# A decoder trunk on one core: the first blocks of x turned one by one, and the first products placed ahead of x's second piece

## What is computed

```python
for l in range(DEPTH):                       # DEPTH 2, D 1024, S 256 rows, float32
    h = rms_norm(x, g_mix[l])
    z = h @ w_in[l]                          # all heads' projections and four gates
    # A: sliding window, 8 query and 2 key heads, rotary; B: latent attention;
    # C: three dilated windows; M: cross-attention into rms_norm(mem)
    ...
    x = x + einsum(gates * y, w_out[l])      # y: the four branches through w_branch
    u = rms_norm(x, g_mlp[l]) @ w_up[l]
    x = x + square(relu(u)) @ w_down[l]
```

## Time and profile before

| | us |
|---|---|
| median of 3 runs | 1241.1 (1241.07 to 1242.55) |
| the profiled execution, whole | 1239.82 |
| its span (what the profile's times count from) | 1238.0 |
| PE busy | 1227.8 |
| DVE busy | 783.5 |
| ACT busy | 701.3 |
| POOL busy | 157.4 |

### The profile page before, as it was taken

One profiled execution on the slowest core, in us unless ns is written; L12 is line 12 of the kernel. 1 busy time (PEld: TensorE's weight loads), 2 busy tenths in 40 slices (PEclk: granted clock), 3 DMA queues, 4 the chain that ended last, 5 costly groups with the idle time before them and its releaser, 6 DMA issues.

```text
span 1238.0 us, 17641 instructions
## 1 busy us (share of the span) xinstructions
PE 1227.8 (99%) x6296; PEld 1018.7 (82%) x6296; DVE 783.5 (63%) x1223; ACT 701.3 (57%) x1087; POOL 157.4 (13%) x127
## 2 busy tenths in 40 slices
PE   8999999999999999999999999999999999999998
PEld 7888888877778888888888888888777888888887
DVE  5857768875556664444567576788655567554454
ACT  6667766654554465545566677666544454644543
POOL 5612334200000000000021223342000000000000
PEclk9999999999999999999999999999999999999999
DMA  9545444455437556565555454444543455555652
GB/s 250 199 135 154 144 136 146 152 167 147 130 112 228 173 178 184 192 180 189 191 162 183 138 156 136 137 136 154 170 134 122 132 196 182 171 191 183 187 186 102
DMA packets 111221, 202.62 MB, mean 164 GB/s; under 512 B 10016, under 2 KB 18720, under 8 KB 111136
## 3 DMA queue, kind: packets, MB, share of 16 engines
q1 hardware_dynamic: 106128, 194.64, 50.7%
q10 hardware_dynamic: 4464, 6.82, 1.7%
q0 software_dynamic: 544, 0.03, 0.1%
HBM read 200.41 MB, written 1.05 MB: 163 GB/s over the span
## 4 chain that ended last, share of the span: by engine, by line
PE 98%; DMA 1%; ACT 0%; issue 0%; ACTq 0%; DVE 0%
PE ps_d L1355 23%; PE ps_d L1357 22%; PE ps_d L1356 22%; PE ps_b L1355 5%; PE ps_b L1356 5%; PE ps_b L1357 5%; PE ps_b L1435 5%; PE ps_b L1389 5%; PE ps_b L1408 4%; PE ps_b L1414 2%; DMA xs<-in_x_dram 1%; PE ps_d L1330 0%; ACT k_c L998 0%; ACT L1042 0%; ACT w_hi L927 0%
## 5 line engine op out<-in xcount | busy, mean ns | idle before, releaser
L1092 DVE TENSOR_TENSOR w_lo<-raw,w_hi 128x1024 fp32r<-128x1024 f32 (+4 forms) x381 | 450.9, 1187 | 309.3 <-ACT w_hi L927 308.0
L927 ACT ACTIVATE w_hi<-raw 128x1024 fp32r<-128x1024 f32 (+4 forms) x381 | 392.1, 1029 | 448.2 <-PE ps_d L1357 349.9
L1355 PE MATMUL ps_d<-w_hi,h_hi 128*128 128x512 f32 (+3 forms) x704 | 285.8, 406 | 0.0
L1357 PE MATMUL ps_d<-w_hi,h_lo 128*128 128x512 f32 (+3 forms) x704 | 267.7, 380 | 0.0
L1356 PE MATMUL ps_d<-w_lo,h_hi 128*128 128x512 f32 (+3 forms) x704 | 266.8, 379 | 0.0
L1355 PE MATMUL ps_d<-w_hi,r_hi 128*128 128x512 f32 (+1 forms) x552 | 219.3, 397 | 0.0
L1357 PE MATMUL ps_d<-w_hi,r_lo 128*128 128x512 f32 (+1 forms) x552 | 214.1, 388 | 0.0
L1356 PE MATMUL ps_d<-w_lo,r_hi 128*128 128x512 f32 (+1 forms) x552 | 213.8, 387 | 0.0
L1355 PEld LDWEIGHTS ps_d<-w_hi,h_hi 128*128 128x128 f32 x704 | 132.6, 188 | 26.1 <-issue 4.6
L1357 PEld LDWEIGHTS ps_d<-w_hi,h_lo 128*128 128x128 f32 x704 | 132.3, 188 | 25.6
L1356 PEld LDWEIGHTS ps_d<-w_lo,h_hi 128*128 128x128 f32 x704 | 132.9, 189 | 18.9
(11 more groups left out here) (156 smaller groups left out, 1277.8 us busy)
## 6 DMA issues: line engine op xcount, KB each, us to landing
raw<-in_w_in_dram SPq DMA_DIRECT2D x151, 512.0 KB, 3.5
raw<-in_w_up_dram SPq DMA_DIRECT2D x64, 512.0 KB, 3.6
raw<-in_w_down_dram SPq DMA_DIRECT2D x64, 512.0 KB, 3.7
raw<-in_w_branch_dram SPq DMA_DIRECT2D x32, 512.0 KB, 3.7
raw<-in_m_w_kv_dram SPq DMA_DIRECT2D x16, 512.0 KB, 4.7
raw<-in_w_out_dram SPq DMA_DIRECT2D x16, 512.0 KB, 3.6
early<-in_b_gate_dram ACTq DMA_DIRECT2D x16, 256.0 KB, 3.6
raw<-in_w_in_dram SPq DMA_DIRECT2D x8, 384.0 KB, 3.5
```

Source lines behind the costliest of these rows:

```text
L927: nc.scalar.activation(w_hi[:, u % RING, 0:kn, 0:cn], raw[:, u % RAW, 0:kn, 0:cn], ACT.Copy).then_inc(hi_split, 1)
L1092: nc.vector.tensor_tensor(w_lo[:, u % RING, 0:kn, 0:cn], raw[:, u % RAW, 0:kn, 0:cn], w_hi[:, u % RING, 0:kn, 0:cn].bitcast(F32), ALU.subt ...
L1355: nc.tensor.matmul(o, hi[:, a["c"], cut], wh, start=a["first"], stop=False)
L1357: last = nc.tensor.matmul(o, lo[:, a["c"], cut], wh, start=False, stop=a["last"])
```

## The change

x's first two blocks are turned and evicted as two items instead of one of two blocks. Its second piece is issued by SyncE, right behind unit 0. All of x's row norms and the memory's get an order number 7 us later; several assumed times change; the first unit of the value projection C0 is cut so that it stands behind the first of query A; and the idle turns are 14 and 8 instead of 24 and 16.

```diff
-    free = {"PE": 0.0, "ACT": 0.0, "DVE": 0.0, "POOL": 14.5, "DMA": 2.4}
+    free = {"PE": 0.0, "ACT": 0.0, "DVE": 0.0, "POOL": 14.5, "DMA": 1.2}
...
-                   since=8.0, q=q, src=source, tt=tt, l=l, **k)
+                   since=13.0, q=q, src=source, tt=tt, l=l, **k)
...
-        def x_turns(c0, c1, dest, gain, came, jobs_needed, order=None):
-            for c in range(c0, c1, 2):
-                turn(("x", jobs_needed), came, c, 2, P, dest, "split", gain, l, order=order,
-                     since=0.0 if jobs_needed else (5.0, 5.6, 8.4)[min(c // 2, 2)])
+        def x_turns(c0, c1, dest, gain, came, jobs_needed, order=None, m=2):
+            for c in range(c0, c1, m):
+                turn(("x", jobs_needed), came, c, m, P, dest, "split", gain, l, order=order,
+                     since=0.0 if jobs_needed else (4.6, 7.2, 9.0)[min(c // 2, 2)])
 
         if l == 0:
-            x_turns(0, half, "h", "g_mix", [], ())
+            x_turns(0, 2, "h", "g_mix", [], (), m=1)
+            x_turns(2, half, "h", "g_mix", [], (), order=-2.0)
             x_turns(half, DC, "h", "g_mix", [], (), order=5.0)
+        axis[0] += 7.0 * (l == 0)
...
+        axis[0] -= 7.0 * (l == 0)
...
-        aq = w_in(COL["aq"], BW, part=(0, half), fine=l == 0)
-        v0 = w_in(COL["c"] + 2 * BW, BW, part=(0, half))
+        aq = w_in(COL["aq"], BW, part=(0, UC), fine=l == 0)
+        v0 = w_in(COL["c"] + 2 * BW, BW, part=(0, UC))
+        aq = w_in(COL["aq"], BW, part=(UC, half), job=aq)
+        v0 = w_in(COL["c"] + 2 * BW, BW, part=(UC, half), job=v0)
...
+                if u == 0:
+                    sp.dma_start(xs[:, :, 2 * P:NW], x_rows[:, :, 2 * P:NW]).then_inc(x_landed[1], 16)
...
-            act.dma_start(xs[:, :, 2 * P:NW], x_rows[:, :, 2 * P:NW]).then_inc(x_landed[1], 16)
...
-            idle_turns(24)
+            idle_turns(14)
...
-                    idle_turns(16)
+                    idle_turns(8)
```

## The result

The changed kernel takes 1244.95 us in the median of its ten runs (lowest 1244.43), the kernel before 1241.33 beside it (1239.91 to 1243.36). One of the ten, at 1742.17 us and a mean granted clock of 0.654, was in a slow state; the median of the other nine is 1244.74. The ratio is 1.003, 95% interval 1.002 to 1.004: slower by 3.4 to 3.6 us. Forecast was 1241.7, range 1239.4 to 1244.9; the result lies at the upper end of the range, by one median just outside and by the other just inside, and six times as far from the kernel before as the +0.6 of the sum. The profiled execution took 1244.44, span 1242.5.

A forecast was written before the change was run, and what follows sets the result against it. PE was taken as the bound, busy 1227.8 of 1238.0 us. Terms of +0.5, +0.4 and -0.3 sum to +0.6 us on a median of 1241.1, giving 1241.7; range 1239.4 to 1244.9.

The forecast's parts named there:

- the sum: Whole kernel: start +0.5, turn of query A +0.4, exponential -0.3, together +0.6 us.
- The turn of query A: At query A's turn on PE: selects from 35.8 us for 6.2, turn ready at 50.75, PE waits 0.4 us.
- rival 2: Pause at 15.2 to 19.0 us: PE's clock falls to half rate, losing 1.6 to 3.2 us; chance 0.14.
- Rival 1: At query A's turn: GpSimd becomes the bound, selects take 9.2 us, PE waits 4.0, time 1245.3 us; chance 0.15.
- The first products: Start of the kernel: first product near 8.4 us instead of 12.14, a lead of 3.7 us.
- Where the lead goes: Before unit 3: frequencies land at 14.2, PE resumes at 19.0 against 18.56; the lead becomes a loss of 0.5 us.
- The exponential near 70: Near 70 us: PE's wait for an exponential falls from 0.8 to 0.5 us, giving 0.3 back.

The follow-up runs named there:

- the second execution of the changed kernel: The changed kernel timed and profiled again without alteration, beside the kernel before: 1244.39 us, ratio 1.0027.
- the kernel with early selects: Changed kernel, selects still ahead of query A's root but directly behind the first memory row's factor, masks' arithmetic behind the angles' second half: 1243.28 us, ratio 1.0015.
- The version with both moves: Changed kernel with query A's root ahead of the selects, and the angles' first half behind low parts of x's blocks 4 to 7: 1240.76 us, ratio 0.9994.

## Why the prediction was wrong

**The step that failed** is in "The turn of query A": "selects from 35.8". I took the time of the split ahead of the masks, 33.9, from the trace of before. But in the new order one square of x and both memory squares stand on ScalarE between 29 and 34.4 us, 3 x 1.05 us that before stood between 16 and 26, and the high part of that split waits behind them. The masks ended at 39.0 instead of 35.6. The second memory factor on GpSimd, behind the same squares, ended at 37.8, so the selects could not have begun at 35.8 even with the masks ready. From there my own numbers hold: 39.2 + 6.1 + 3.45 + 5.35 (48.84 to 54.19) gives 54.1, against 54.2. That the squares are the reason is read from the traces, not from a run that moves them alone. PE being late can be ruled out: in the second execution of the changed kernel ScalarE went through this stretch from 27.70 on without a wait for PE, PE was 2.6 us earlier, and the selects still began at 38.63. The move of the norms stood in the diff; I followed it to GpSimd's order and not to ScalarE's. So the turn was ready 3.5 us later than forecast (54.2 against 50.75). The wait for it was 2.78 us in the second execution but only 0.85 in the first, against 0.4, since there PE was late as well, by a second term that the sum had put at nothing: the half clock behind the pause, left to rival 2 with 0.14, which measured 2.7.

The selects' own length was right, 6.1 against 6.2, and in part by luck: the short ones of before stood beside low parts, and the new place has no low parts. That they are as short with VectorE standing still is shown only by the 3.68 us in the old kernel.

**Rival 1** was right in place and sign, near in the time (1245.3, against 1244.95) and in the time the turn is ready (54.3, against 54.2), and wrong in its reason, so the nearness is luck. It took selects of 9.2 us from 35.8; they took 6.1, as in my forecast, and were late. Its wait of 4.0 was 0.85 and 2.78. Taking the order back brought 3.2 us (0.9998 against 1.0027), putting it into the old kernel cost 7.6.

**The first products**: 9.07 instead of 8.4. Unit 1 landed at 7.2, and its high part stands ahead of the first eviction (L932 at 7.26 with a wait of 2.52 for its load). The lead was 3.1, not 3.7.

**Where the lead goes**: right. Frequencies used from 14.37 (14.2), PE on at 19.40 (19.0), +0.84 instead of +0.5. But this term alone says little of the time: moving the angles out of the way won 0.6, 0.4 or nothing (-1.5) in three settings, each time with overlapping intervals. The lead is lost for a second reason as well, which I had only as a bound: unit 3's data lands no earlier than before (split at 13.63, before 13.15), and with the angles away PE goes on at 17.21, where the bound was 17.1. Loads and splits, not PE, set the pace up to there.

**Rival 2**, the clock: it did what was said (half rate from 19.4 for 6 us), and 2.7 us is within the 1.6 to 3.2 that were said, if nothing covers it. The changed kernel is as slow without it: the other profiled execution had full clock there and the same turn within 0.6 us. It shows in the profile of the kernel with early selects. Of this the Trainium skill, TensorE: Matmul & The Clock Gate, Part 1, says that the same kernel shows different counts of slow matmuls from run to run. The trace agrees: the half clock lay at 9 to 12.5 in one execution of the changed kernel and at 19.4 to 25.3 in another.

**The clock in the comparison.** In the first series of experiments, the kernel before took 1239.5 to 1240.2 us in its runs at a mean granted clock of 1.000, and 1242.5 to 1243.0 in those at 0.997; the changed kernel 1243.8 and 1243.9, and 1244.7 to 1246.0. So at equal clock the difference is 4.2 us at 1.000 (from 1239.65 to 1243.85) and some 2.9 at 0.997. The profile of before, which the sum was made against, was one of the former, and 1.3 below its median. The version with both moves has 1240.4 to 1240.8 at 1.000: at equal clock it is some 1.1 above the kernel before, and its lower median goes with 6 of its 11 runs being at 1.000, against 5 of 30. A mean clock is itself an outcome of the pauses, so this tells where the medians differ and not why.

**The exponential near 70**: the wait of 0.77 is gone, and one of 0.38 stands at 81.22 for a scaling (L1199). From the turn of query A to the eight turns it is 26.89 us, before 29.87 - 2.88 = 26.99: -0.1 instead of -0.3.

**The sum of the profiled executions**: +0.84 at the pause; from 19.4 to 25.3 matmuls every 0.43 us instead of 0.23, 5.9 x (1 - 0.23/0.43) = +2.7; wait +0.85; exponential -0.1: 4.3, against 4.5 measured.

## What to carry to other kernels

An order number or an assumed time of a planner moves work on every engine that the item's chain passes; when such a number changes, read each engine's order for what now stands ahead of the chain that comes next, and do not take a start time from the old trace if its predecessors have moved. A lead won at the start is worth only what the next common landing leaves of it: look for that place before counting it. Where a wait and a clock stretch lie ahead of the same late chain, only one of them counts, and mending that one uncovers the other.

## What the runs showed of the hardware

GpSimd's 11 selects took 3.68 us with VectorE standing still, 5.6 to 6.6 beside a reduction and splits, and 9.2 to 10.2 beside scaling and rotation. The same work differs by a factor of 2.5 to 2.8 with what VectorE does beside it. By tile, in ns (minimum, median, maximum), with VectorE still, in the kernel before with its selects ahead:

```profile
L913 POOL TENSOR_SCALAR_AFFINE_SELECT mask<-mask x11: 288/394/402, 42.0 to 45.2; 128x256 bf16<-128x256 bf16 x7, 128x128 bf16<-128x128 bf16 x4
```

In the changed kernel:

```profile
L912 POOL TENSOR_SCALAR_AFFINE_SELECT mask<-mask x11: 285/393/1378, 39.2 to 44.9; 128x256 bf16<-128x256 bf16 x7, 128x128 bf16<-128x128 bf16 x4
```

The median did not move, only some of them meet a neighbour. Query A's root of 16 columns took 2.9 us at best and 3.8 to 3.9 beside splits.

Half clock followed each of the pauses of 3.07 to 3.21 us behind 16 us (in four executions), but not the pause of 3.42 us at 6.6 us in the kernel before. Waits ahead of the first product went both ways: 2.57 to 2.67 us with full clock behind them in three executions, 2.57 with half clock in another. So did those at the turn of query A: full clock behind 2.65 us, half clock behind 2.78 and 5.52. The kernel with both moves, whose waits for low parts in the first 20 us were 1.6 and 1.1 us, had full clock up to 90 us. What decides between these stays open.
